# The third layer's differential attention in pair phases, high and low weight parts at set places, and ada rows ahead of a layer

## What is computed

```python
h = rms_norm(x, norm_g[i]) * (1.0 + sc[:, None]) + sh[:, None]   # sh, sc, gt from silu(c) @ ada_w[i]
u, z = jnp.split(h @ w_in, [n_mix_cols], axis=-1)
# A: grouped attention, 16 heads on 4; B: neighbourhood attention with a bias; C, the third layer:
p = jax.nn.softmax(logits, axis=-1)
a = p[:, :, 0] - lam * p[:, :, 1]
o = jnp.einsum("bhqk,bkhd->bqhd", a, v)
o = rms_norm(o, subln_g) * (1.0 - lambda_init)
x = x + gt[:, None] * ((o * jax.nn.silu(z)) @ w_out)
```

## Time and profile before

| what | value |
|---|---|
| median of three runs | 2190.47 us (2190.22 to 2192.97) |
| the profiled execution | 2195.91 us |
| its span, first to last instruction | 2194.1 us |
| PE busy | 1974.0 us, 90% |
| DVE, ACT, POOL busy | 1199.5, 1098.0, 985.2 us |
| granted TensorE clock, mean | 0.946 |
| the second block's four layers | from about 940 to 2194 us |
| third layer's attention, eight chunks and the start of W_out | 1742 to 1948 us |

### The profile page before, as it was taken

How to read it: one execution, slowest core, us unless ns; L and a number is a source line. 1 busy time by engine, 2 the same in 40 slices (tenths; PEclk the granted TensorE clock), 3 DMA queues, 4 the chain that set the end, 5 groups by cost and what they waited for, 6 DMA issues and landing times.

```text
span 2194.1 us, 39543 instructions
## 1 busy us (share of the span) xinstructions
PE 1974.0 (90%) x14720; PEld 1675.1 (76%) x14720; DVE 1199.5 (55%) x2584; ACT 1098.0 (50%) x2101; POOL 985.2 (45%) x616
## 2 busy tenths in 40 slices
PE   6899899998999899969998899899879989977897
PEld 5798789988898899946776697666569666656676
DVE  5854556657654466435775304677340766723574
ACT  5353465444543665454554526454443555644563
POOL 0474468303754485024453443344234545533563
PEclk8899999998999999979999999899999989989998
DMA  7343556564444565543112422322232211123222
GB/s 258 113 148 106 176 173 188 183 200 131 132 126 148 178 194 185 176 158 105 50 49 78 163 87 77 103 72 62 93 125 87 70 66 49 49 91 119 80 87 59
DMA packets 72994, 262.93 MB, mean 120 GB/s; under 512 B 8048, under 2 KB 10224, under 8 KB 72560
## 3 DMA queue, kind: packets, MB, share of 16 engines
q1 hardware_dynamic: 71536, 256.31, 36.5%
q0 software_dynamic: 1280, 4.20, 0.6%
HBM read 259.43 MB, written 1.05 MB: 119 GB/s over the span
## 4 chain that ended last, share of the span: by engine, by line
PE 67%; DVE 14%; issue 6%; ACT 6%; POOL 5%; DMA 1%; SPq 0%; DVEq 0%; ACTq 0%; POOLq 0%
PE gemm L494 16%; PE gemm L495 15%; PE gemm L496 15%; PE score L852 2%; DVE pr L1940 2%; DVE small L1903 2%; PE stat L739 2%; POOL w_parts L327 2%; PE obank L925 1%; PE gemm L792 1%; POOL rot L2124 1%; PE gemm L793 1%; PE gemm L794 1%; PE gemm L702 1%; ACT pr L1460 1%
## 5 line engine op out<-in xcount | busy, mean ns | idle before, releaser
L327 POOL TENSOR_TENSOR w_parts<-ring,w_parts 128x1024 fp32r<-128x1024 f32 x280 | 672.8, 2406 | 709.7 <-ACT w_parts L1112 698.7
L1112 ACT ACTIVATE w_parts<-ring 128x1024 fp32r<-128x1024 f32 x364 | 382.6, 1054 | 136.0 <-PE gemm L496 63.3
L494 PE MATMUL gemm<-g_hi,w_parts 128*128 128x256 f32 x1344 | 396.1, 295 | 28.5 <-DVE w_parts L327 10.7
L494 PE MATMUL gemm<-h_hi,w_parts 128*128 128x512 f32 (+1 forms) x928 | 379.8, 409 | 14.9 <-ACTq L1352 6.8
L495 PE MATMUL gemm<-g_lo,w_parts 128*128 128x256 f32 x1344 | 385.7, 287 | 0.0
L496 PE MATMUL gemm<-g_hi,w_parts 128*128 128x256 f32 x1344 | 385.1, 287 | 0.0
L495 PE MATMUL gemm<-h_lo,w_parts 128*128 128x512 f32 (+1 forms) x928 | 352.0, 379 | 0.0
L496 PE MATMUL gemm<-h_hi,w_parts 128*128 128x512 f32 (+1 forms) x928 | 351.5, 379 | 0.0
L494 PEld LDWEIGHTS gemm<-g_hi,w_parts 128*128 128x128 f32 x1344 | 265.4, 197 | 47.6 <-issue 24.0
L495 PEld LDWEIGHTS gemm<-g_lo,w_parts 128*128 128x128 f32 x1344 | 264.8, 197 | 0.1
L496 PEld LDWEIGHTS gemm<-g_hi,w_parts 128*128 128x128 f32 x1344 | 264.3, 197 | 0.0
(11 more groups left out here) (328 smaller groups left out, 3972.3 us busy)
## 6 DMA issues: line engine op xcount, KB each, us to landing
ring<-wall SPq DMA_DIRECT2D x478, 512.0 KB, 3.7
r<-nbias POOLq DMA_DIRECT2D x16, 256.0 KB, 3.0
cst<-consts SPq DMA_DIRECT2D x1, 2037.0 KB, 13.4
r<-x_t SPq DMA_DIRECT2D x1, 1024.0 KB, 5.7
x<-ctx_t SPq DMA_DIRECT2D x1, 1024.0 KB, 15.7
y_t<-x SPq DMA_DIRECT2D x4, 256.0 KB, 3.0
cst<-consts SPq DMA_DIRECT2D x1, 303.5 KB, 3.1
x<-pos SPq DMA_DIRECT2D x1, 128.0 KB, 2.1
```

What stands on the lines that cost most here:

```text
L327: eng.tensor_tensor(w_lo[:, at, :, :], ring[:, t % RING, :, :], w_hi[:, at, :, :].bitcast(F), ALU.subtract)\
L494: pe.matmul(out, w[0][:, k, :], x[0], start=start, stop=False)
L1112: act.activation(w_hi[:, at, :, :], ring[:, t % RING, :, :], ACT.Copy).then_inc(S["hi_ready"], 1)
```

## The change

It touches the second block alone, in four ways, and adds or removes no weight tile.

1. Kind C takes the order of the other kinds: scores of a pair, transposes of the pair before in row halves (eight of 64 rows instead of four of 128, into tb and t2), four pieces of GEMM, values. DVE and ACT copy half of the columns each (`first_columns`, `second_columns`, 128x256 elements). `output`, `output_squares`, `subln`, `q_start`, `q_end`, `q_rms` and `gate_out` stand at new places in their engines' orders, and so do the last transposes, values and outputs among W_out's first products. GEMM pieces are cut into 12 instead of 6 parts a chunk.
2. In kinds A and B ACT makes the high part of the q tile after next (`qz_tile(L, 2 * c + 3)`) behind the exponentials of the first pair of each chunk, and POOL waits for the first normalised pair of the chunk before its low part.
3. Ahead of each layer all `FILL_RMS` ada rows are multiplied before the value products, into banks ob and tb, and copied out by ACT behind the h parts; their columns follow the first value pair, in the same banks.
4. The high parts of the first layer's first two value tiles move from the last row copy of the first block to behind the reciprocal root of the first layer.

```diff
+        def qz_tile(L, i):
+
+            return AT["qz", L] + i + (4 if i >= 4 else 0) if FILL_SLOT[L] else AT["qz", L] + i + 1
+
+        def outs_before(g):
+
+            return max(0, (g - 2) // 3)
+
+        def half_columns(g, i):
+
+            return pt[:, g % 2, :].rearrange("p (j i n) -> p j i n", j=4, i=2)[:, :, i, :]
...
-                run(ada_row())
+                for r in range(FILL_RMS[L]):
+                    run(ada_row((ob, tb)[r]))
...
-                        for _ in range(FILL_RMS[L] - 1):
-                            run(ada_row())
-                        for _ in range(FILL_RMS[L]):
-                            ada_columns()
+                        for r in range(FILL_RMS[L]):
+                            ada_columns((ob, tb)[r])
...
-                def to_keys(c, u):
+                def pair_to_keys(c, u):
 
                     U = c * NU + u
-                    pe.wait_ge(S["comb_ready"], U // 2 + 1)
-                    if c == 0 and not turned_at:
-                        pe.wait_ge(S["ss_used"], kbase(L) + nk - 1)
-                    src = eb[:, (U // 2) % 2, :]
-                    transpose_bank(lambda j: src[:, j * P:(j + 1) * P], 4)
-                    turned_at[c, u] = n["t"]
-
-                def pair_to_keys(c, u):
-
-                    U = c * NU + u
-                    pe.wait_ge(S["p_normed"], pbase(L) + U + 2)
+                    if kind == "C":
+                        pe.wait_ge(S["comb_ready"], U // 2 + 1)
+                    else:
+                        pe.wait_ge(S["p_normed"], pbase(L) + U + 2)
                     if c == 0 and u == 0:
                         pe.wait_ge(S["ss_used"], kbase(L) + nk - 1)
                     pe.wait_ge(S["t_read"], n["t"])
+                    heads = [eb[:, U // 2 % 2, :]] if kind == "C" else [pr[:, (U + hh) % 3, :] for hh in range(2)]
                     for j in range(4):
-                        for hh in range(2):
+                        for hh, src in enumerate(heads):
                             for i in range(2):
                                 r, o = slice(i * HD, (i + 1) * HD), (4 * hh + j) * HD
-                                ins = pe.transpose((tb, t2)[i][:, o:o + HD], pr[r, (U + hh) % 3, j * P:(j + 1) * P], ident[r, r])
-                                if j == 3 and hh == 1:
+                                ins = pe.transpose((tb, t2)[i][:, o:o + HD], src[r, j * P:(j + 1) * P], ident[r, r])
+                                if j == 3 and hh == len(heads) - 1:
                                     ins.then_inc(S["t_ready"], 1)
                     n["t"] += 2
                     turned_at[c, u + 1] = n["t"]
...
-                    spot, parts = 0, NU if kind == "C" else 2 * NU
+                    spot, parts = 0, 2 * NU
...
-                            values_both(last[0], last[1] // 2)
-                    for u in range(NU) if kind == "C" else ():
-                        past = [(c, u)] + past[:3]
-                        if u % 2 == 0:
-                            scores(c, u)
-                        gemm_part()
-                        if past[2] and closes(kind, us[past[2][1]]):
-                            to_keys(*past[2])
-                        if past[3] and closes(kind, us[past[3][1]]):
-                            values(*past[3])
+                            if kind == "C":
+                                values(last[0], last[1] + 1)
+                            else:
+                                values_both(last[0], last[1] // 2)
                         if kind == "C" and u == OT and c:
                             out_to_features(c - 1)
-                        if u == NU - 2 and c + 1 < KC:
-                            q_sums(c + 1)
-                last = [(KC - 1, u) for u in range(NU) if closes(kind, us[u])]
-                if kind == "C":
-                    to_keys(*last[-1])
-                    values(*last[-2])
...
                 w_out_part(0, 0, 3)
+                pair_to_keys(KC - 1, NU - 2)
                 if kind == "C":
-                    values(*last[-1])
+                    w_out_part(0, 3, 4)
+                    values(KC - 1, NU - 1)
+                    w_out_part(0, 4, KC - 1)
+                    w_out_part(1, 0, 2)
+                    out_to_features(KC - 1)
+                    w_out_part(1, 2, KC - 1)
                 else:
-                    pair_to_keys(KC - 1, NU - 2)
-                w_out_part(0, 3, KC - 1)
-                if kind == "C":
-                    out_to_features(KC - 1)
-                else:
+                    w_out_part(0, 3, KC - 1)
                     values_both(KC - 1, NU // 2 - 1)
-                w_out_part(1, 0, KC - 1)
+                    w_out_part(1, 0, KC - 1)
...
-                    ada_row_out()
+                    ada_row_out(AHEAD if first else 0)
...
+                if L == 0:
+                    hi_parts(n["tile"] + 1)
                 n["tile"] += 2
-                ada_row_out(0)
...
-                        hi_parts(n["tile"])
+                        hi_parts(n["tile"] + 4)
                 high(KC - 1)
+                for r in range(FILL_RMS[L]):
+                    ada_row_out(0, (ob, tb)[r])
...
+                def second_columns(c, u):
+
+                    g = (c * NU + u) // 2
+                    act.wait_ge(S["t_ready"], tbase(L) + 2 * g + 2 + outs_before(g))
+                    act.activation(half_columns(g, 1), t2[:, 0:T].rearrange("p (j n) -> p j n", j=4), ACT.Copy).then_inc(S["t_read"], 1)
...
+                        if kind == "C" and u == OT and c:
+                            subln(c - 1)
                         if last[0] >= 0:
-                            second_keys(*last)
+                            if kind == "C":
+                                second_columns(*last)
+                            else:
+                                second_keys(*last)
+                        if kind == "C" and u == 2 and c:
+                            output_squares(c - 1)
                         exponential(c, u)
                         exponential(c, u + 1)
+                        if kind != "C" and u == 0:
+                            hi_parts(qz_tile(L, 2 * c + 3))
...
+                def first_columns(c, u):
+
+                    g = (c * NU + u) // 2
+                    dve.wait_ge(S["t_ready"], tbase(L) + 2 * g + 2 + outs_before(g))
+                    dve.tensor_copy(half_columns(g, 0), tb[:, 0:T].rearrange("p (j n) -> p j n", j=4)).then_inc(S["t_read"], 1)
...
+                        if kind == "C":
+                            done = (c, u - 3) if u >= 4 else (c - 1, u + 3)
+                            if done[0] >= 0:
+                                output(*done)
                         biggest(c, u)
                         biggest(c, u + 1)
                         if last[0] >= 0:
-                            first_keys(*last)
-                        if u == OT and c:
+                            if kind == "C":
+                                first_columns(*last)
+                            else:
+                                first_keys(*last)
+                        if kind != "C" and u == OT and c:
                             gate_out(c - 1)
                         if NU == 6 and u == 4 and c + 1 < KC:
                             q_end(c + 1)
-                        normalise(c, u)
-                        normalise(c, u + 1)
+                        if kind == "C":
+                            combine(c, u + 1)
+                        else:
+                            normalise(c, u)
+                            normalise(c, u + 1)
                         if u == 2 and c + 1 < KC:
                             q_start(c + 1)
                             if NU == 4:
                                 q_end(c + 1)
                         if u == NU - 2 and c + 1 < KC:
                             q_rms(c + 1)
+                        if kind == "C" and u == OT and c:
+                            gate_out(c - 1)
...
+                    output(KC - 1, NU - 3)
+                    first_columns(KC - 1, NU - 2)
+                    output(KC - 1, NU - 1)
...
-                    split_to(qz_tile(2 * c + 1) if c else AT["k", L] + 1)
+                    if c and kind != "C":
+                        pool.wait_ge(S["p_normed"], pbase(L) + (c - 1) * NU + 2)
+                    split_to(qz_tile(L, 2 * c + 1) if c else AT["k", L] + 1)
```

98 lines of the change are left out of this document (27 added, 71 removed).

## The result

| | before | after |
|---|---|---|
| median of four runs | 2190.34 us | 2165.29 us |
| lowest to highest | 2189.76 to 2192.97 | 2163.78 to 2166.02 |
| the profiled execution, its span | 2195.9, 2194.1 us | 2165.1, 2163.3 us |
| PE, DVE, ACT, POOL busy | 1974.0, 1199.5, 1098.0, 985.2 us | 1957.9, 1204.4, 1095.0, 980.1 us |
| granted clock, mean | 0.946 | 0.951 |

The median is 25.05 us lower. The ratio of the times is 0.9877, with a 95% interval of 0.9861 to 0.9894, which is 26.9 us less (23.2 to 30.4). The forecast was 29.3 us, 2161 us, in a range of 2146 to 2180. So sign and range held, and the forecast median is 4.3 us too low. Its terms did less well than its sum: the third layer gave about half of what was forecast, other places gave more.

What follows compares the result with a forecast made beforehand. PE was the engine to watch, its waits differing by layer. Savings of 9.0 + 3.7 + 1.8 + 1 + 13.8 = 29.3 us gave 2166.6 us profiled, 2161 us median, in a range of 2146 to 2180.

Steps and rivals of the forecast that it cites:

- Low parts, first and second layer: First and second layer's chunks: an earlier high part lets POOL's low part start earlier, shortening the transposes' waits; 9.0 us saved.
- The bank wait of the second chunk: First and second layer: falls by the 1.05 us the high part took ahead of the bank's read; 1.5 us taken.
- The last layer's end: Eighth chunk to the end: output chunk 2's low part is ready in time; 2.7 + 2.6 - 1.6 = 3.7 us saved.
- Ada rows: Ahead of layers two to four: the wait for a bank ahead of the columns goes; 1.8 us saved, bound 0 to 2.4.
- First layer's rows: First layer's start: squares 3.2 us earlier, q's GEMM later, 2.7 lost; 1 us gain taken, from -2 to +5.
- The third layer: New order of its chunks: steady chunks 4, first 1.2, second 2.3, last 6.3; 13.8 us saved, from 6 to 25.
- The sum of DVE's chain: Third layer's steady chunks: DVE's chain from one power to the next sets 21.9 us a chunk, against 22.7 before.
- rival (c): Third layer: a whole low part falls on a combine in two phases of each chunk; slower, 2202 us; chance 0.08.
- (a): Third layer: the wait moves, DVE's chain stays as long; 13.8 becomes 4, time 2171 us; chance 0.22.
- (b): Third layer: PE sets the pace, chunks take 19.8 to 20.3 us; 12 us more gain, 2149 us; chance 0.15.
- a wait of 1.2 us for gate_out's bank: Third-layer chunks, a sign of being right: PE's first transposes wait about 1.2 us for bank tb, inside the 21.9.
- collisions, chunks over 23 us: Third layer, a sign of being wrong: chunks over 23 us would show collisions.

Runs made afterwards that it cites:

- the first experiment: The kernel before with only the low parts timed in layers 1, 2 and 4, third layer and ada rows as before: 2181.43 us, ratio 0.9946.
- the last experiment: The changed kernel with the first layer's two high parts back at the first block's last row copy: 2162.95 us, ratio 0.9873.
- the second experiment: The change without its third-layer part (low parts timed, ada rows moved, third layer in its old order): 2169.75 us, ratio 0.9911.

## Why the prediction was right, and where it wasn't

*Low parts, first and second layer* (forecast 9.0). Right in its mechanism and a little small: 3.3 and 7.9 us by the first experiment. A second-layer chunk lost 1.25 us instead of 1.1, and the last one 2.9. The bank wait of the second chunk gave 1.1 in the first layer and nothing in the second, 1.5 forecast. The prediction said that POOL's new wait costs nothing, and nothing shows that it does. What it left out is that the wait itself makes the gain of the first layer, whose chunks are some 3 us longer without it; I still held the opposite before that experiment.

*The last layer's end* (3.7). Measured 3.9, 2.8 in the first experiment, and 3.4 with the reach alone undone. The parts of the term were off, though: the wait for the low part fell by 3.6 us where 2.7 were forecast, and the early low part cost 3.1 us of wait for DVE, not 1.6. PE's waits together are 10.2 us before and after, so all of the gain is PE's busy time, 31.9 instead of 35.7 us at the higher clock, where 2.6 were forecast (and the forecast's own figures, 5.0 less 2.7, give 2.3). That the sum came out right is luck.

*Ada rows* (1.8). Measured 2.5 ahead of the layers. In the same comparison the second layer's first chunk ran at a clock of 0.91 instead of 0.77 and took 19.7 instead of 22.4 us. No term had that, and its cause stays open: the kernel with the rows undone takes 19.8 there.

*First layer's rows* (+1, from -2 to +5). The moves were forecast to a few tenths: squares 3.2 us shorter (measured 3.2), the eighth row tile 17.7 us behind the sums (measured 17.9), value products at 18.2 (18.9), q's GEMM at 33 (33.0). But the loss of 2.7 us didn't come, since q's GEMM behind the wait of 5.93 us had been running at a clock of 0.74 and now ran at 1.00: 11.3 against 8.6 us. The term is 3.5. The step left out is the time behind a wait. And the view of before couldn't show what the last experiment did: the late high parts cost 9.6 us there, which the other gains of the new order hide. So of the four parts of the change, the move of the high parts lost 6.6 us net by the traces.

*The third layer* (13.8). Measured 7.1 in the two executions, 8.3 against the second experiment. The sum of DVE's chain, 21.9 us, came close to the 21.48 that a chunk takes where the clock is up, but by luck. With the low part timed a chunk takes 20.65 us, so the chain without its 0.3 for a low part, 21.6, was at least 0.9 too long, and a collision that the chain didn't have filled the gap. Its 0.3 us stood on the cosine product, which was never held (0.66 to 0.68 us in every chunk of this layer). The two ends of the layer: chunk 0 gave 1.2 as forecast (0.9 of it also in the old order, in the second experiment), chunk 1 3.4 instead of 2.3, but the last chunk takes 30.3 us and not 26.8, with 2.6 us for a combine under a low part and 4.2 for the row's copy. The step that failed is where POOL's low part falls in a chunk, and so its price. I had put it beside the cosine product and given it 0.3 us, because "they follow the power and the scaling". It follows the scaling's power by 0.2 us, and that is when the second combine runs. That is rival (c) at half its size: one low part a chunk on a combine instead of two. With it PE waits 1.46 us a chunk, which the chain of 21.48 contains; and behind that wait comes what no term had, a stretch at the low clock that costs 3.5, 2.7 and 1.5 us in three chunks, 7.7 in all. Without that, the five chunks would have taken 107.4 us, 6.2 less than the 113.6 before; with it they take 115.1, 1.6 more.

Of the rivals, (a), the wait moves, is what the steady chunks did, though by another cause than the chain's length. (b) came true only once the low part was timed: 19.98 us, PE's own need, was forecast as 19.8. Of the prediction's signs, a wait of 1.2 us for gate_out's bank was forecast and isn't there (0.3), and its sign of being wrong by collisions, chunks over 23 us, did show: three of the five steady chunks took 24.99, 24.18 and 23.01 us.

*The sum.* That the total is right is luck, since the terms' errors cancel: the third layer 6.7 too much, the second layer 3.2, the first layer's start 2.5 and the rest some 0.7 too little. That leaves 29.0 against 29.3. The miss of 4.3 us in the median goes with the saving "taken over as it is" from an execution that was 5.6 us slower than its median, and 29.3 lies inside the interval of the ratio. What decided the third layer was POOL's low part beside the combine's last operation, which the prediction had in rival (c) alone: 2.72 instead of 0.75 us. The Trainium skill's rule on shared interfaces (GPSIMD Engine Reference, "Specifications") names an operation with two SBUF inputs, which the combine's last one is, and the trace agrees, with these two times.

## What to carry to other kernels

When a change reorders one engine's queue, list for each long operation of the engine that shares its memory path what runs beside it now, and price every collision in the new order; letting POOL wait for the DVE operation that must not be disturbed cost no time that shows here and gave some 3 us in one layer and, together with an earlier high part, over 10 in another. Price a wait of the engine that sets the pace together with the stretch behind it: here a wait of 1.5 us was followed by a stretch at half the clock in most of the third layer's steady chunks. And ask what a later low part holds: behind it the wait for a weight tile grew by 3.7 us where 4.3 were won in the third layer's last chunk, and at the first layer's start 9.6 us were lost for 3.0 won.

## What was not expected of the hardware

- A PE wait of 1.46 us, once a chunk in work that is otherwise without a gap, was followed by matmuls at the low clock level (a granted clock of 0.86 or 0.93 over the chunk) in 22 of 35 chunks; two waits of 0.8 us a chunk were so in none of 15. The same wait at the same place had it in one execution and not in the next (chunk 2: 25.0 and 21.9 us). Nor does the length alone decide: a wait of 1.9 us for a bank in the layer's second chunk was followed by the full clock in the changed kernel (1.00 over that chunk) and by a low stretch in the kernel with the low part timed (0.93).
- A DVE operation with two SBUF inputs, 128x512, takes 0.75 us alone, 1.64 with the last 1.1 us of a POOL product beside it and 2.72 with nearly a whole low part; maxima out of PSUM keep their 0.69 us, also beside a low part.
